# A three-layer hybrid network on one core: the recurrence stage of layers 1 and 2 in another order, and products that nobody reads

## The reference, cut to what matters

```python
for l in range(DEPTH_2):                      # layers 1 and 2 of the kernel
    h = rms_norm_2(x, attn_norm_g[l])
    pa, pb, pc = split_sizes(h @ w_in[l], (A_PROJ, B_PROJ, C_PROJ))
    ya = rwkv7_mixer(pa, ...)                 # recurrence, 4 heads of 64
    yb = dilated_mixer(pb, cos_b, sin_b)      # attention, 4 heads of 64 ("B heads", 0 to 3)
    yc = mla_mixer(pc, cos_c, sin_c, ...)     # attention from latents, 4 heads ("C heads", 4 to 7)
    x = x + jnp.concatenate([ya, yb, yc], axis=-1) @ w_out[l]
    h = rms_norm_2(x, ffn_norm_g[l])
    x = x + (jax.nn.silu(h @ ffn_w_gate[l]) * (h @ ffn_w_up[l])) @ ffn_w_down[l]
...
def step(state, inp):                         # inside rwkv7_mixer, over the 256 tokens
    r_t, w_t, k_t, v_t, kk_t, b_t = inp
    sa = jnp.einsum('bhvk,bhk->bhv', state, kk_t)
    state = (state * w_t[:, :, None, :] - sa[..., None] * b_t[:, :, None, :]
             + v_t[..., None] * k_t[:, :, None, :])
    y = jnp.einsum('bhvk,bhk->bhv', state, r_t)
```

## Time and profile before

| | |
|---|---|
| median of 3 runs (lowest, highest) | 1105.38 us (1104.76, 1110.9) |
| profiled execution: device time, its span | 1106.32 us, 1104.4 us |
| mean granted clock of PE | 0.954 |
| PE busy | 1052.7 us (95%) |
| DVE, ACT busy | 684.1 us (62%), 503.8 us (46%) |
| DMA | 156.41 MB, 142 GB/s over the span |

### The profile page before, as it was taken

The page is one execution under the profiler, slowest core; times in us unless marked ns, Lnnn a source line. Parts: engine busy times, 40 slices in busy tenths (PEclk is TensorE's granted clock), DMA queues, the critical chain, the costliest instruction groups (busy, mean ns, idle before and its releaser), DMA issues. The chain is left out here.

```text
span 1104.4 us, 20079 instructions
## 1 busy us (share of the span) xinstructions
PE 1052.7 (95%) x8728; PEld 989.1 (90%) x8728; DVE 684.1 (62%) x1079; ACT 503.8 (46%) x663; POOL 4.1 (0%) x9
## 2 busy tenths in 40 slices
PE   5999989999997998999999999999899999999996
PEld 5898889999997997769999999998776799999996
DVE  5867476775567877444665555579653456655554
ACT  5475464444436543233644443466233455444332
POOL 0000000000000000000000000000000000000000
PEclk9999999999999999579999999999985899999999
DMA  8444334555452322021455555533220135555531
GB/s 315 153 140 162 115 144 165 191 182 199 165 184 85 135 87 80 37 77 60 184 191 191 181 179 182 185 120 115 78 78 33 44 115 191 191 191 188 179 130 39
DMA packets 23736, 156.41 MB, mean 142 GB/s; under 512 B 2576, under 2 KB 3776, under 8 KB 6112
## 3 DMA queue, kind: packets, MB, share of 16 engines
q1 hardware_dynamic: 21600, 151.70, 38.2%
q10 hardware_dynamic: 1840, 2.50, 0.7%
q0 software_dynamic: 208, 0.92, 0.3%
HBM read 154.05 MB, written 1.06 MB: 140 GB/s over the span
## 5 line engine op out<-in xcount | busy, mean ns | idle before, releaser
L441 PE MATMUL bank<-h_hi,w_hi 128*128 128x256 f32 x1480 | 427.9, 289 | 26.8 <-DVE w_lo L2045 11.1
L1455 DVE TENSOR_TENSOR w_lo<-raw,w_hi 128x2048 fp32r<-128x2048 f32 (+3 forms) x144 | 323.5, 2251 | 179.6 <-ACT w_hi L1040 178.3
L441 PE MATMUL bank<-h_lo,w_hi 128*128 128x256 f32 x1480 | 422.4, 285 | 0.0
L441 PE MATMUL bank<-h_hi,w_lo 128*128 128x256 f32 x1480 | 422.1, 285 | 0.0
L441 PEld LDWEIGHTS bank<-h_hi,w_hi 128*128 128x128 f32 x1480 | 287.5, 194 | 32.3 <-issue 19.2
L1040 ACT ACTIVATE w_hi<-raw 128x2048 fp32r<-128x2048 f32 (+3 forms) x144 | 269.2, 1873 | 91.5 <-PE bank L441 86.4
L441 PEld LDWEIGHTS bank<-h_lo,w_hi 128*128 128x128 f32 x1480 | 287.7, 194 | 1.0 <-issue 0.7
L441 PEld LDWEIGHTS bank<-h_hi,w_lo 128*128 128x128 f32 x1480 | 287.6, 194 | 0.0
L441 PE MATMUL bank<-mix_hi,w_hi 128*128 128x256 f32 x720 | 205.3, 285 | 2.5 <-DVE mix_lo L1437 2.0
L441 PE MATMUL bank<-mix_lo,w_hi 128*128 128x256 f32 x720 | 203.7, 283 | 0.0
L441 PE MATMUL bank<-mix_hi,w_lo 128*128 128x256 f32 x720 | 203.7, 283 | 0.0
(11 more groups left out here) (299 smaller groups left out, 935.8 us busy)
## 6 DMA issues: line engine op xcount, KB each, us to landing
raw<-in_w SPq DMA_DIRECT2D x136, 1024.0 KB, 4.8
raw<-in_w SPq DMA_DIRECT2D x5, 512.0 KB, 3.7
raw<-in_w SPq DMA_DIRECT2D x2, 896.0 KB, 4.5
raw<-in_w SPq DMA_DIRECT2D x2, 768.0 KB, 4.2
cst<-in_consts SPq DMA_DIRECT2D x1, 1314.0 KB, 12.7
x<-in_x SPq DMA_DIRECT2D x2, 512.0 KB, 6.0
arena<-bias_rows ACTq DMA_DIRECT2D x1, 1024.0 KB, 6.1
out<-arena ACTq DMA_DIRECT2D x4, 256.0 KB, 2.0
```

The lines of the kernel that those rows point to most:

```text
L441: last = pe.matmul(dst, w[a](k), act[b](k), start=start and i == 0 and j == 0, stop=stop and i == n - 1 and j == 2, skip_group_check=loose)
L1455: dve.tensor_tensor(w_lo[:, s, 0:n], raw[:, s, 0:n], w_hi[:, s, 0:n].bitcast(F32), ALU.subtract)\
```

## The change

**PE.** The transpose "inv0" is issued between the halves of projection 7, level 1's y products behind it, level 1's back products between the halves of projection 8 (`between`). For levels 2 to 5 `beside_inverse` has two halves, one before and one after the back products: (2,0) b_rot and up 0, (2,1) up 1, (3,0) up 2, (3,1) k_rot and up 3, (4,0) up 4 and 5, (4,1) q_rot and up 6, (5,0) head 0, (5,1) head 1. Levels 5 and 6 have their old order. Head 0 waits for rotation 1 and up 6; for the rotated C queries (`c_rope`) only head 4 waits.

**ACT.** The hi split of ukv comes before the hi copies of the latents (was after); that of out 1 after level 4 (was after head 4); up 4 is copied with level 4.

**DVE.** Projection 7 is evacuated before level 1's BT. The lo split of uq comes before level 1's subtractions, the latents' lo halves and projection 8's evacuation after them; the rotations 0, 1, 2 and the lo splits of ukv and out 0 are spread over the halves; the gate operations stand behind the logits of head 0, rotation 3 behind those of head 1. The lo split of out 1 comes after s1 (was after head 4), that of out 2 after `center(1)` (was after head 5, before s1).

**Unread products.** `keep_busy` issues fp32 products of 128 x 256 into bank 7 whose results nobody reads: 13 at the start, on zeros that a new DVE memset writes, and 6 behind each of layer 0's two `norm_sum` "mixed" and "fed".

```diff
+        filler = rope[:, 0, :]
...
-        AFTER_LEVEL = {1: ("ukv", 0), 2: ("out", 0)}
-        AFTER_HEAD = {4: ("out", 1), 5: ("out", 2)}
+        AFTER_LEVEL = {2: ("out", 0), 4: ("out", 1)}
...
+            def keep_busy(n, operand, dst):
+
+
+                for _ in range(n):
+                    pe.matmul(dst, operand[:, 0:P], operand[:, 0:T], start=True, stop=True)
+
...
-            def project(l, *which, begun=False):
+            def project(l, *which, begun=False, between=lambda: None):
...
+                            if t:
+                                between()
...
-                project(l, 7)
-
                 Xm, XT, BT, Y = INV["x"], INV["xt"], INV["bt"], INV["yy"]
-                for q in range(2):
-                    pe.wait_ge(V.sem, V.at(l, "inv0", q))
-                    for m in range(4):
-                        for h in HALVES:
-                            last = pe.matmul(quads(q)[h, m, 0:64], XT[h, 4 * q + m, :], IDENT[h, h],
-                                             start=True, stop=True)
-                    last.then_inc(M.sem, M.mark(l, "inv0", q))
-                project(l, 8)
-                for n in range(1, 6):
+
+                def turn_inverse():
                     for q in range(2):
-
-                        pe.wait_ge(V.sem, V.at(l, "inv_bt", n, q))
-                        pe.wait_ge(A.sem, A.at(l, "inv0", q)) if n == 1 else pe.wait_ge(V.sem, V.at(l, "inv_x", n - 1, q))
-                        for m in range(4 * q, 4 * q + 4):
+                        pe.wait_ge(V.sem, V.at(l, "inv0", q))
+                        for m in range(4):
                             for h in HALVES:
-                                last = pe.matmul(quads(q)[h, m % 4, 0:64], BT[h, m, :], Xm[h, m, :],
+                                last = pe.matmul(quads(q)[h, m, 0:64], XT[h, 4 * q + m, :], IDENT[h, h],
                                                  start=True, stop=True)
-                        last.then_inc(M.sem, M.mark(l, "inv_y", n, q))
-                    beside_inverse(l, n)
+                        last.then_inc(M.sem, M.mark(l, "inv0", q))
+
+                project(l, 7, between=turn_inverse)
+                def back_products(n):
                     for q in range(2):
                         pe.wait_ge(A.sem, A.at(l, "inv_y", n, q))
                         for m in range(4 * q, 4 * q + 4):
...
                                 last = pe.matmul(blocks(quads(q)[h, m % 4, 0:64], n, 0), XT[h, m, :],
                                                  blocks(Y[h, m, :], n, 0), start=True, stop=True)
                         last.then_inc(M.sem, M.mark(l, "inv_z", n, q))
-                    if n >= 5:
-                        attention(l, 2 * n - 9)
+
+                for n in range(1, 6):
+                    for q in range(2):
+
+                        pe.wait_ge(V.sem, V.at(l, "inv_bt", n, q))
+                        pe.wait_ge(A.sem, A.at(l, "inv0", q)) if n == 1 else pe.wait_ge(V.sem, V.at(l, "inv_x", n - 1, q))
+                        for m in range(4 * q, 4 * q + 4):
+                            for h in HALVES:
+                                last = pe.matmul(quads(q)[h, m % 4, 0:64], BT[h, m, :], Xm[h, m, :],
+                                                 start=True, stop=True)
+                        last.then_inc(M.sem, M.mark(l, "inv_y", n, q))
+                    if n == 1:
+                        project(l, 8, between=lambda: back_products(1))
+                        continue
+                    beside_inverse(l, n, 0)
+                    back_products(n)
+                    beside_inverse(l, n, 1)
 
                 for q in range(2):
                     pe.wait_ge(V.sem, V.at(l, "inv_x", 5, q))
...
                         last = pe.matmul(quads(q)[64:P, m % 4, 0:64], gram[0:64, m, 0, 64:P], Xm[0:64, m, :],
                                          start=True, stop=True)
                     last.then_inc(M.sem, M.mark(l, "inv_y", 6, q))
-                beside_inverse(l, 6)
+                attention(l, 2)
...
-                if n == 1:
-
+                if (n, half) == (2, 0):
                     pe.wait_ge(V.sem, V.at(l, "in", 7))
                     pe.wait_ge(A.sem, A.at(l, "rkv"))
                     pe.wait_ge(A.sem, A.at(l, "kb_turned"))
                     pe.matmul(bank[6][:, :], C("rot_b"), B2["bq"].rearrange("p a b -> p (a b)"), start=True, stop=True)
                     pe.matmul(bank[7][:, :], C("rot_b"), B2["bk"].rearrange("p a b -> p (a b)"), start=True, stop=True)\
                         .then_inc(M.sem, M.mark(l, "b_rot"))
-                if n == 2:
                     pe.wait_ge(V.sem, V.at(l, "c_lo"))
+                    pe.wait_ge(V.sem, V.at(l, "in", 8))
                     up(0)
+                if (n, half) == (2, 1):
                     up(1)
-                if n == 3:
-
+                if (n, half) == (3, 0):
+                    up(2)
+                if (n, half) == (3, 1):
                     pe.wait_ge(V.sem, V.at(l, "rotated", 0))
                     pe.matmul(bank[6][:, 0:T], C("dup")[0:64, :], B2["krope"][0:64, :], start=True, stop=True)
                     pe.matmul(bank[6][:, T:2 * T], C("dup_rot")[0:64, :], B2["krope"][0:64, :], start=True, stop=True)\
                         .then_inc(M.sem, M.mark(l, "k_rot"))
-                    for i in range(2, 5):
-                        up(i)
-                if n == 4:
+                    up(3)
+                if (n, half) == (4, 0):
+                    up(4)
+                    up(5)
+                if (n, half) == (4, 1):
                     pe.wait_ge(V.sem, V.at(l, "rotated", 1))
                     pe.matmul(bank[7][:, :], C("rot_c"), b["qr"].rearrange("p a b -> p (a b)"), start=True, stop=True)\
                         .then_inc(M.sem, M.mark(l, "q_rot"))
-                    up(5)
                     up(6)
-                if n >= 5:
-                    attention(l, 2 * n - 10)
+                if n == 5:
+                    attention(l, half)
...
                 if i == 0:
+                    pe.wait_ge(V.sem, V.at(l, "rotated", 1))
+                    pe.wait_ge(A.sem, A.at(l, "up", 6))
+                if i == 4:
                     pe.wait_ge(V.sem, V.at(l, "c_rope"))
-                    pe.wait_ge(A.sem, A.at(l, "up", 6))
                 if i == 8:
 
                     pe.wait_ge(V.sem, V.at(l, "b_lo"))
                 attend(l, i, 8, scores, value, out_bank)
 
+            pe.wait_ge(V.sem, V.at("filler"))
+            keep_busy(13, filler, bank[7][:, 0:T])
...
                     norm_sum(l, "mixed")
+                    keep_busy(6, cst, bank[7][:, 0:T])
                 ffn(l)
                 if l == 0:
                     norm_sum(l, "fed")
+                    keep_busy(6, cst, bank[7][:, 0:T])
...
+                        hi_of(CHUNK[l, "ukv", 0])
...
-                    for i in {2: (0, 1), 3: (2, 3, 4), 4: (5, 6)}.get(n, ()):
+                    for i in {2: (0, 1), 3: (2, 3), 4: (4, 5, 6)}.get(n, ()):
...
-                    if c == 0:
-                        hi_of(CHUNK[l, *AFTER_HEAD[4]])
                     if c:
                         square_of(0)
                     attend(l, 5 + 3 * c, 8)
                     if c == 0:
-                        hi_of(CHUNK[l, *AFTER_HEAD[5]])
+                        hi_of(CHUNK[l, "out", 2])
...
-                def beside_inverse(n):
-                    if n == 1:
-
-                        evacuate(l, 7, B2["bk"])
+                def beside_inverse(n, half):
+
+                    if (n, half) == (1, 0):
                         after_a(l, "rkv")
                         for t in range(2):
                             dve.scalar_tensor_tensor(b["cqn"][:, t, :], B2["cq"][:, t, :], Par(f"qn{l}", t), b["rq"],
                                                      ALU.mult, ALU.mult)
                         dve.scalar_tensor_tensor(b["ckvn"], B2["ckv"], Par(f"kvn{l}", 0), b["rkv"], ALU.mult, ALU.mult)\
                             .then_inc(V.sem, V.mark(l, "c_n"))
+                        lo_of(CHUNK[l, "uq", 0])
+                    if (n, half) == (1, 1):
+                        latents_lo()
                         evacuate(l, 8, B2["bv"], token_major=True)
-                    if n == 2:
+                    if (n, half) == (2, 0):
                         after_m(l, "b_rot")
                         rotate(0, B2["bq"], B2["bq"], pairs(6), 0)
+                    if (n, half) == (2, 1):
+                        lo_of(CHUNK[l, "ukv", 0])
+                    if (n, half) == (3, 0):
                         rotate(1, B2["bk"], B2["bk"], pairs(7), 0)
-                    if n == 3:
+                    if (n, half) == (3, 1):
                         after_m(l, "k_rot")
                         rotate(2, b["kro"], bank[6][:, 0:T], bank[6][:, T:2 * T], 2)
-                    if n == 4:
-
+                    if (n, half) == (4, 0):
```

(32 more changed lines are left out.)

3 lines of the change are left out of this document (removed).

## The result

| | before | after |
|---|---|---|
| median, us | 1105.93 (1104.76 to 1110.9, 4 runs) | 1090.55 (1086.55 to 1093.96, 4 runs) |
| ratio | | 0.9841, 95% interval 0.9812 to 0.987 |
| profiled execution: time; span | 1106.32; 1104.4 | 1086.55; 1084.7 |
| PE busy | 1052.7 (95%) | 1051.8 (97%) |
| sum of the half-clock time in the span | 103.4 us | 73.0 us |

The account below looks back on a forecast made before the run. PE was taken as the bound, through its waits and its time at 1.2 GHz. 11.2 us for two layers, 1.8 at the start and 0.3 at the norms made 13.3, thus 1092 us; own range 1086 to 1098, with rivals 1074 to 1103.

Parts of the forecast that it names:

- the unread products: At the start and behind layer 0's two norms: 1.8 us gained by a faster start, 0.3 at the norms.
- Levels 1 to 4: Inverse, each layer: PE's waits (5.7 us) and half-speed time (1.5) go, less 0.3 and 1.0 of costs: 5.9 us gained.
- ACT's split of out 0: Level 3: this hi split stands ahead of the copy of Y; up(2) covers all but 0.2 to 0.4 us, charged 0.3.
- back(5) waits for ACT: Level 5: ACT's split of out 1 delays the copy of Y, a new PE wait of 0.8 us per layer.
- rotate 3's 1.3 us: Head 1: at full clock PE would wait some 1.3 us for DVE's query rotation; taken as 0, half clock being expected.
- The clock falls later, within level 5 or 6: Levels 5 and 6: the fall comes some 3.5 us of work later, gaining 1.5 us per layer (bounds 0 and 15).
- The transposes: Heads: if transposes do not count as busy for the clock, level 5's 1.5 us per layer would go, forecast 1095.
- Probabilities of head 5: End of the heads: with out 2's split moved from before s1, they follow 0.7 to 0.8 us sooner; gain 0.8.
- Split of out 2 behind center(1): Stage's end: the split delays the mix's lo halves and w_out(0, 4..7), 1.8 us lost per layer (bounds 1.5 and 3.3).
- Rival 2: Levels: waits are refilled behind other ACT or DVE instructions, levels give 1 to 2 us each, 1103 us; chance 0.14.
- rival 3: Between the levels: shorter dense runs let the clock fall in level 2 or 3 until the recurrence, 1115 us; chance 0.08.
- Rival 1: Levels 5 and 6: the clock holds through most of the stage, 10 us more per layer, 1072 us; chance 0.15.

Follow-up runs that it names:

- o1_out1: The changed kernel with ACT's hi split of out 1 moved back from behind level 4 to behind head 4; 1092.56 us, ratio 0.9846 to the kernel before.
- c1: The changed kernel with six dense unread products each ahead of back(5) and in head 1, head 0 waiting for rotation 2; 1075.48 us, ratio 0.9699 to before.
- h1: The changed kernel with six dense unread products at each of five places per layer in levels 5 and 6, head 0 waiting for rotation 2; 1073.77 us, ratio 0.9694.
- t1_tail: The changed kernel with DVE's lo split of out 2 moved from behind center(1) to just ahead of it; 1086.86 us, ratio 0.9805 to the kernel before.
- r1: The changed kernel without its unread products at the start and behind the two norms; 1091.20 us, ratio 0.9842 to the kernel before.
- b1: The changed kernel with out 2's lo split ahead of center(1), out 1's hi split behind head 4, rotate 3 in level 4, gate operations behind head 3; 1082.21 us.
- c2: The changed kernel with six dense unread products in each of heads 0, 2 and 3 only, head 0 waiting for rotation 2; 1077.95 us, ratio 0.9725 to before.

## Why the prediction was right, step by step

On the median 15.4 us came for 13.3 forecast, but two misses of opposite sign stand in that: the unread products gave nothing for 2.1, and levels and clock gave more than was counted. That they nearly cancel is luck. The steps below are read from the profiled execution, whose 19.7 us are 6.4 above the forecast; it is the fastest of four.

- **Levels 1 to 4: right.** 5.9 us per layer were forecast; 6.8 came in layer 1 (1.9 to 8.7) and 6.9 in layer 2 (9.9 to 16.9). All waits went, also the 0.3 us charged for ACT's split of out 0. Waits and clock piece make 7.4, so ten dense runs instead of five cost some 0.5 us and not 1.0, if nothing else did.
- **back(5) waits for ACT: right in size (0.8 forecast, 0.83), wrong as a price.** o1_out1 takes it away and gains nothing, since DVE's chain lay just under it. I had rotate 3's 1.3 us in the text for the case of full clock (0.77 in o1, 1.07 in c1), but not the gate operations, behind which PE waits 0.64 us in after and 1.46 in o1.
- **The clock falls later, within level 5 or 6: right; its worth too small.** 1.5 us per layer forecast, 3.5 measured in layer 1 (37.6 to 30.7 us of half-clock time) and 5.2 in layer 2 (41.0 to 30.7), beside short falls: the one at 498 before has made room for another at 495, behind the new wait, and the one at 863 in layer 2 is gone. With these it is the term that carried the profiled execution furthest past the forecast; for the median no trace tells. In the other traces of the new order without unread products in levels 5 and 6 the long fall lasts 27.3 to 34.1 us.
- **The transposes.** The Trainium skill (TensorE: Matmul & The Clock Gate, Part 4: PE-mode transpose) says that they do not count as busy in the same way, from which 1095 followed. The fall came later all the same, and heads 4 and 5 hold 1.00 in h1 with three transposes each; but no run separates transposes from the products beside them.
- **Probabilities of head 5: 0.8 forecast.** PE's wait there fell from 1.65 to 0.36 us in layer 1 and from 1.44 to 1.02 in layer 2: 0.9 on the mean.
- **Split of out 2 behind center(1): right.** 1.8 us lost forecast, 1.7 measured in both layers (13.1 to 11.4, 21.4 to 19.7), and in layer 1 the clock's 1.5 as well (11.4 to 9.9), inside the bound of 3.3. t1_tail shows it by taking it away.
- **The unread products: wrong.** 2.1 us forecast, 0 measured (r1 against after, ratios 0.9842 and 0.9841; each is uncertain by 0.3%, 3 us). The start's 1.8 us was there in the profiled trace and in two more of twelve; in the other nine it was 0.1 to 1.1. At the norms +0.3 was forecast with a bound of -0.2; behind the first of them -1.2 us came in seven of ten traces, because the fall moved from ahead of the wait for h_lo to behind it. Over both norms seven of ten traces are level with before and three 1.2 us longer. I had named that wait and not priced the clock behind it.
- **Rivals.** Rival 2 (waits refilled) and rival 3 (fall in level 2 or 3) did not occur. Rival 1 did not occur either, yet its price was about right: held by unread work at five places, which also fills the waits, the clock gives 1073.8, for 1072 forecast. Of what I held against it, the argument that weighed most (this kind of work does not lift the clock, so it will not hold it) was the flaw: it does not lift it, but with the waits filled it holds it. That the clock fell all the same was thus forecast in part for a wrong reason; the waits, my other reason, were the better one.

## What to carry to other kernels

When the granted clock is at half for tens of microseconds with PE busy all the time, look at the waits just ahead of the fall, and at where the next dense products come: a few microseconds of unread products in those waits can pay back several times their length (c1: 2.0 us of them in layer 1, and some 8 us less per layer). Before filling a wait, look for a second one right behind it: there the filling gained nothing (the norms). When one engine's wait is taken away, first write down when the next engine in line would have been ready; and put a long side job where its engine is idle now, not just behind the operation that ends the idle time.

## What the runs showed of the hardware

- Holding and lifting differ: products of 64 rows and columns and the heads' products keep 2.4 GHz over more than 20 us and a wait of 1.29 us (h1 from 453 to 477 us), and do not lift it from 1.2 GHz in 27 to 41 us without a single wait (before, after, b1, c1). With six dense products in heads 2 and 3 it was back after 3.4 and 6.8 us in the profiled execution of c2, but hardly in all its executions.
- The same instructions with the same wait of 1.07 us fell in one layer and not in the other (c1). Waits of 2.05 us ahead of dense products were followed by a short fall 11 times in 16. The short falls in these traces were 3.4 us of half clock, worth 1.7 us, or twice that; their number is much of what differs from trace to trace.
- At the program's start the granted-clock row reads 1.00 in 10 to 15 us both in r1, where products come 0.22 us apart, and in after, where they come 0.12 apart. There the pace has to be read, not the row.
